# A Hyena convolution's spectra and inverses regrouped by even and odd times in a two-layer diffusion block

## The reference

```python
h = x * (1.0 + sc1) + sh1
q, k, v, z_hy, gate_a, gate_b = jnp.split(h @ lp['w_in'], SPLITS, axis=-1)
...
def bidir_long_conv(u, h, bias):
    L, C = u.shape[1], u.shape[2]
    g = jnp.concatenate([h[:, 0], jnp.zeros((1, C), jnp.float32), h[:0:-1, 1]], axis=0)
    U = jnp.fft.rfft(u, n=2 * L, axis=1)
    G = jnp.fft.rfft(g, n=2 * L, axis=0)
    y = jnp.fft.irfft(U * G[None], n=2 * L, axis=1)[:, :L]
    return y + u * bias
```

## Time and profile before

| what | value |
|---|---|
| median of 3 runs | 2062.82 us (2062.6 to 2062.84) |
| the profiled execution, its own time | 2061.39 us |
| its span, first to last instruction | 2059.6 us |
| mean granted TensorE clock | 0.992 of full |
| TensorE busy | 2016.4 us (98%), 13030 matmuls |
| VectorE busy | 1142.6 us (55%) |
| ScalarE busy | 747.6 us (36%) |
| GpSimd busy | 184.0 us (9%) |
| DMA | 207.07 MB, 101 GB/s over the span |

### The profile page before, as it was taken

How to read it: one execution, slowest core, us unless ns; L and a number is a source line. 1 busy time by engine, 2 the same in 40 slices (tenths; PEclk the granted TensorE clock), 3 DMA queues, 4 the chain that set the end, 5 groups by cost and what they waited for, 6 DMA issues and landing times.

```text
span 2059.6 us, 30339 instructions
## 1 busy us (share of the span) xinstructions
PE 2016.4 (98%) x13030; PEld 1917.8 (93%) x13030; DVE 1142.6 (55%) x1682; ACT 747.6 (36%) x1103; POOL 184.0 (9%) x202
## 2 busy tenths in 40 slices
PE   8999999999999999999999999999999999999997
PEld 3589998999989999999998999899998999999996
DVE  6416457777556767776545454863246433233435
ACT  3354453522264321333244443452226332133323
POOL 0120001200141000000031000120015000000011
PEclk9999999999999999999999998999999999999998
DMA  8331112254313335434322101222221212212121
GB/s 313 143 124 64 39 62 92 88 179 165 125 59 123 138 133 197 178 126 154 105 71 82 65 21 60 98 77 82 82 83 47 90 63 71 90 65 79 63 71 52
DMA packets 37726, 207.07 MB, mean 101 GB/s; under 512 B 4326, under 2 KB 7959, under 8 KB 18904
## 3 DMA queue, kind: packets, MB, share of 16 engines
q1 hardware_dynamic: 31192, 185.04, 25.1%
q0 software_dynamic: 3312, 13.35, 1.8%
q10 hardware_dynamic: 3088, 6.75, 0.9%
HBM read 196.98 MB, written 8.14 MB: 100 GB/s over the span
## 4 chain that ended last, share of the span: by engine, by line
PE 90%; DVE 4%; ACT 3%; issue 1%; DMA 1%; SPq 0%; POOL 0%; ACTq 0%; DVEq 0%
PE gemm_psum L609 50%; PE gemm_psum L639 15%; PE gemm_psum L662 3%; PE gemm_psum L682 3%; PE gemm_psum L622 3%; PE aux_psum L749 3%; PE aux_psum L802 2%; PE gemm_psum L788 2%; PE aux_psum L730 2%; PE gemm_psum L551 2%; PE gemm_psum L515 1%; PE aux_psum L738 1%; ACT h_src_rows L1174 1%; PE aux_psum L772 1%; DMA ada_early<-in_ada 1%
## 5 line engine op out<-in xcount | busy, mean ns | idle before, releaser
L609 PE MATMUL gemm_psum<-h_hi,w_hi 128*128 128x322 f32 x2144 | 497.2, 313 | 0.3
L609 PE MATMUL gemm_psum<-h_hi,w_lo 128*128 128x322 f32 x2144 | 493.5, 311 | 0.0
L609 PE MATMUL gemm_psum<-h_lo,w_hi 128*128 128x322 f32 x2144 | 492.1, 311 | 0.0
L609 PEld LDWEIGHTS gemm_psum<-h_hi,w_hi 128*128 128x128 f32 x2144 | 362.5, 189 | 4.4 <-issue 3.1
L609 PEld LDWEIGHTS gemm_psum<-h_lo,w_hi 128*128 128x128 f32 x2144 | 362.7, 189 | 0.0
L609 PEld LDWEIGHTS gemm_psum<-h_hi,w_lo 128*128 128x128 f32 x2144 | 362.2, 189 | 0.0
L1574 DVE TENSOR_TENSOR w_lo<-w_raw,w_hi 128x2048 fp32r<-128x2048 f32 (+3 forms) x130 | 251.3, 1933 | 198.7 <-ACT w_hi L1104 197.7
L1104 ACT ACTIVATE w_hi<-w_raw 128x2048 fp32r<-128x2048 f32 (+3 forms) x130 | 209.6, 1612 | 170.1 <-PE gemm_psum L639 65.6
L1562 DVE CUSTOM_DVE_ANT_0 aux_psum<-w_raw,cond_by_row 128x1024 f32<-128x1024 f32 x160 | 190.9, 1256 | 6.9 <-DMA w_raw<-in_ada_t 6.4
L1707 DVE SCALAR_TENSOR_TENSOR x<-gemm_psum,mod,x 128x128 f32<-128x128 f32 (+2 forms) x144 | 55.4, 434 | 157.8 <-PE gemm_psum L639 128.0
L639 PE MATMUL gemm_psum<-act_hi,w_lo 128*128 128x322 f32 x616 | 141.9, 311 | 0.0
(11 more groups left out here) (337 smaller groups left out, 3276.0 us busy)
## 6 DMA issues: line engine op xcount, KB each, us to landing
w_raw<-in_w_up SPq DMA_DIRECT2D x44, 1024.0 KB, 4.8
w_raw<-in_ada_t SPq DMA_DIRECT2D x40, 1024.0 KB, 4.7
w_raw<-in_w_down SPq DMA_DIRECT2D x32, 704.0 KB, 4.2
w_raw<-in_w_gate SPq DMA_DIRECT2D x16, 1024.0 KB, 4.7
w_raw<-in_w_z SPq DMA_DIRECT2D x12, 1024.0 KB, 4.7
w_raw<-in_w_out SPq DMA_DIRECT2D x8, 1024.0 KB, 4.7
g_kept<-g_rows_out POOLq DMA_DIRECT2D x10, 512.0 KB, 2.9
ada_early<-in_ada SPq DMA_DIRECT2D x4, 1024.0 KB, 20.4
```

Of the source, the lines that this page charges most:

```text
L609: last = mm(gp[:, 2 * (t % 2) + hf, 0:HALF], w[:, off + P * kk:off + P * (kk + 1)], moving(kk, lo)[:, hf * HALF:(hf + 1) * HALF], start=kk ...
```

## The change

The latent times are taken as four blocks by half (t below or from 256) and parity. The even-frequency inverses give 256 times. For the odd frequencies, only 4k + 1 is transformed directly, once from the even times (pair 3) and once from the odd times (pair 4), with two blocks each; their sum and difference are the two sets of odd spectra. The filter's odd spectra are combined in the same way, on GpSimd before they are stored. After the product with the filter, the two sets are again combined into an even-time and an odd-time part. Inverses are 256 columns wide and accumulate into two halves of a bank: a part that is equal for t and t + 256, and one that turns its sign; VectorE joins them. Chunk I1 is gone, and F1 comes ahead of I0. F0 has 12 blocks, F1 10 (with the context's inverse). The spectra 3 and 4 both run ahead of all latent inverses.

The diff, cut to its core:

```diff
-F0_BLOCKS, F1_BLOCKS = 14, 16
+F0_BLOCKS, F1_BLOCKS = 12, 10
-        + [("F", 0), ("pa", 0), ("I", 0), ("F", 1), ("I", 1)]
+        + [("F", 0), ("pa", 0), ("F", 1), ("I", 0)]
...
+    chunk_done[gF:gG] = [("usp_mm", 6), ("pa_mm", EARLY), ("usp_mm", 10), ("linv_mm", 4)]
-    EARLY_BANKS = [(1, 2), (1, 0), (1, 0), (0, 2)]
+    EARLY_BANKS = [(1, 2), (1, 0), (1, 2), (1, 0)]
-    G_V = [(0, 1), (2, 3), (4, 5), (6, 7, 8, 9), (6, 7, 8, 9)]
+    G_V = [(0, 1), (2, 3), (4, 5), (6, 8), (7, 9)]
...
+    def u_cols(b):
+        at = L0 + 2 * P * ((b - 1) // 2) + (b - 1) % 2
+        return CTX if b == 0 else slice(at, at + 2 * P - 1, 2)
...
-                    at = 512 * (2 * ((pair_ - 1) % 2) + o)
+                    at = 256 * (2 * (pair_ - 1) + o)
-                        last = mm(ax[:, j, :], y[:, ys, o, P * j:P * (j + 1)], w[slot][:, at:at + 512],
+                        last = mm(out(j), y[:, ys, o, P * j:P * (j + 1)], parts(w[slot][:, at:at + 256]),
...
+            for n in (2, 3):
+                pe.wait_ge(sem["pa_out"], due("pa_out", n - 1))
+                attn_projected(n)
+            pe.wait_ge(sem["w_split"], due("w_split", gF1 + 1))
             pe.wait_ge(sem["y_ready"], due("y_ready", 2))
...
+            pe.wait_ge(sem["us_rest"], due("us_rest", 4))
+            spectrum(3, U_V[3])
+            spectrum(4, U_V[4])
             pe.wait_ge(sem["w_split"], due("w_split", gI + 1))
             pe.wait_ge(sem["pa_out"], due("pa_out", 4))
+            for pair_ in range(1, PAIRS):
+                inverse(pair_, slot_of(gI), pair_ == 1, pair_ == PAIRS - 1)
...
+            act.wait_ge(sem["usp_mm"], due("usp_mm", 4))
+            split(gF1)
...
+                if p_ == 2:
+                    for o in range(2):
+                        act.wait_ge(sem["usp_mm"], due("usp_mm", 7 + o))
+                        run(ureg[:, 2 * o, :], spec_bank(6 + o), ACT.Copy).then_inc(sem["odd_out"], raised("odd_out"))
+                    split(gG)
...
+            split(gI)
+            dve.wait_ge(sem["cinv_mm"], due("cinv_mm", 1))
...
+            for o in range(2):
+                dve.wait_ge(sem["odd_out"], due("odd_out", o + 1))
+                dve.wait_ge(sem["usp_mm"], due("usp_mm", 9 + o))
+                first = ureg[:, 2 * o, :]
+                TT(ureg[:, 2 * o + 1, :], first, spec_bank(8 + o), ALU.subtract).then_inc(sem["usp_out"], raised("usp_out"))
+                dve.wait_ge(sem["usp_out"], now("usp_out"))
+                TT(first, first, spec_bank(8 + o), ALU.add).then_inc(sem["usp_out"], raised("usp_out"))
...
+            for at in range(2):
+                gr, gi = gsp[:, at, 0, :], gsp[:, at, 1, :]
+                ur, ui = ureg[:, at, :], ureg[:, 2 + at, :]
...
+                for to, a, b in ((prod[:, 0, :], ur, gr), (prod[:, 1, :], ui, gi), (us[:, 0, :], ur, gi), (us[:, 1, :], ui, gr)):
+                    TT(to, a, b, ALU.mult).then_inc(sem["dve_order"], raised("dve_order"))
+                dve.wait_ge(sem["dve_order"], now("dve_order"))
+                TT(ur, prod[:, 0, :], prod[:, 1, :], ALU.subtract).then_inc(sem["dve_order"], raised("dve_order"))
+                TT(ui, us[:, 0, :], us[:, 1, :], ALU.add).then_inc(sem["dve_order"], raised("dve_order"))
+            dve.wait_ge(sem["dve_order"], now("dve_order"))
+            for at, op in ((0, ALU.add), (1, ALU.subtract)):
+                for to, n in ((us, 2), (prod, 0)):
+                    TT(to[:, at, :], ureg[:, n, :], ureg[:, n + 1, :], op).then_inc(sem["y_src"], raised("y_src"))
+            for p_ in (3, 4):
+                for o in range(2):
+                    lo(ylo[:, Y_SLOT[p_], 1 - o, :], (us, prod)[o][:, p_ - 3, :], yhi[:, Y_SLOT[p_], 1 - o, :],
+                       "y_hi", 2 * p_ + o + 1, "y_ready")
             split(gG)
...
             for j in range(NHY):
-                STT(xu[:, j, LAT], xu[:, j, LAT], parc("hy_bias", j), ax[:, j, :], ALU.mult, ALU.add)\
+                rows = xu[:, j, LAT].rearrange("p (a t b) -> p a b t", a=2, b=2)
+                same, turned = (ax[:, j, 256 * a:256 * (a + 1)].rearrange("p (b t) -> p b t", b=2) for a in range(2))
+                for a in range(2):
+                    STT(rows[:, a], rows[:, a], parc("hy_bias", j), same, ALU.mult, ALU.add)\
+                        .then_inc(sem["dve_order"], raised("dve_order"))
+                dve.wait_ge(sem["dve_order"], now("dve_order"))
+                for a, op in ((0, ALU.add), (1, ALU.subtract)):
+                    TT(rows[:, a], rows[:, a], turned, op).then_inc(sem["dve_order"], raised("dve_order"))
...
+        def g_combine(l):
+            if l:
+                pool.wait_ge(sem["g_spill"], 16 * PAIRS)
+            pool.wait_ge(sem["gsp_out"], 10 * l + 6)
+            for o in range(2):
+                G.tensor_tensor(g_first[:, o, :], gst[:, 3, o, :], gst[:, 4, o, :], ALU.add).then_inc(sem["g_halves"], 1)
+            pool.wait_ge(sem["g_halves"], 4 * l + 2)
+            for o in range(2):
+                G.tensor_tensor(gst[:, 4, o, :], gst[:, 3, o, :], gst[:, 4, o, :], ALU.subtract).then_inc(sem["g_halves"], 1)
+            pool.wait_ge(sem["g_halves"], 4 * l + 4)
```

More of the change, by code:

```diff
@@ L345, in _program @@
         h2T = sb("h2T", [P, NT], F32, s)
-        feat = sb("feat", [FEAT, NT], F32, s)
+        with ExitStack() as s2:
+            feat = sb("feat", [FEAT, NT], F32, s2)
+        g_first = sb("g_first_half", [P, 2, HY_W], F32, s)
         dreg = sb("d_block", [P, 2, HY_W], F32, s)
@@ L547, in g_spectrum @@
                 for kb, pl in enumerate(places):
[L548 removed]
+                    blk = 4 * (pair_ % 3) + 2 * o + kb
                     cols_ = slice(P * blk, P * (blk + 1))
@@ L784, in spectrum @@
                 for kb, pl in enumerate(places):
-                    blk = (4 * pair_ + 2 * o + kb) if pair_ < 3 else (8 * (pair_ - 3) + 4 * o + kb)
+                    blk = 4 * (pair_ % 3) + 2 * o + kb
                     cols_ = slice(P * blk, P * (blk + 1))
@@ L794, in inverse, with out @@
             ys = Y_SLOT[pair_]
+            parts = lambda ap: ap if pair_ < 3 else ap.rearrange("p (a t) -> p a t", a=2)
+            def out(j):
+                if pair_ < 3:
+                    return ax[:, j, 256 * (pair_ - 1):256 * pair_]
+                return ax[:, j, :].rearrange("p (a b t) -> p a b t", a=2, b=2)[:, :, pair_ - 3, :]
             for o in (1, 0):
@@ L1323, in _ @@
                     early_row(1)
-                    split(gI)
                 if p_ == 1:
@@ L1835, in _ @@
             split(gA)
-            for p_ in range(PAIRS):
+            for p_ in range(3):
                 gr, gi = gsp[:, G_SLOT[p_], 0, :], gsp[:, G_SLOT[p_], 1, :]
@@ L1871, in _ @@
-                if p_ == 3:
-                    split(gI1)
+                if p_ == 0:
+                    split(gF1)
+            split(gI)
+            dve.wait_ge(sem["cinv_mm"], due("cinv_mm", 1))
+            for j in range(NHY):
+                STT(xu[:, j, CTX], xu[:, j, CTX], parc("hy_bias", j), ax[:, 2, P * j:P * (j + 1)],
+                       ALU.mult, ALU.add).then_inc(sem["cinv_out" if j == 3 else "dve_order"], raised("cinv_out" if j == 3 else "dve_order"))
+            for o in range(2):
[5 more added lines that the diff above has]
+                TT(first, first, spec_bank(8 + o), ALU.add).then_inc(sem["usp_out"], raised("usp_out"))
@@ L2084, in _ @@
                         h_lo(0, h, d)
-                        if h == 0 and d % 2:
-                            g_spill(1, d // 2 + 1)
+                        if d == KD - 1:
+                            if h:
+                                g_combine(1)
+                            for n in (1, 2) if h else (3, 4):
+                                g_spill(1, n)
             pool.wait_ge(sem["h_ready"], due("h_ready", 2 * KD))
@@ L2189, in _dft_constants @@
     k4 = np.arange(P)
+    two = [2 * np.arange(P) + b for b in range(2)]
     lat = []
@@ L2192, in _dft_constants @@
         re, im = forward(4 * k4 + add, DEC_SEQ // 2, N)
+        br, bi = back(4 * k4 + add, DEC_SEQ // 2, N)
         if add == 0:
@@ L2195, in _dft_constants @@
             im[:, 0] = np.cos(np.pi * np.arange(DEC_SEQ // 2))
-        lat += [re[:P], re[P:], im[:P], im[P:]]
-        br, bi = back(4 * k4 + add, DEC_SEQ, N)
-        if add == 0:
             br[0] /= 2
-            bi[0] = np.cos(np.pi * np.arange(DEC_SEQ)) / N
-        i0 += [br, bi]
-    f0 = ctx + lat + cinv
-    f1 = []
-    for o in range(2):
-        fr = 2 * (P * o + np.arange(P)) + 1
-        re, im = forward(fr, DEC_SEQ, N)
-        f1 += [m[P * b:P * (b + 1)] for m in (re, im) for b in range(4)]
-        i1 += list(back(fr, DEC_SEQ, N))
+            bi[0] = np.cos(np.pi * np.arange(DEC_SEQ // 2)) / N
+        lat += [m[rows] for m in (re, im) for rows in two]
+        i0 += [m[:, cols] for m in (br, bi) for cols in two]
+    f0 = ctx + lat
+    re, im = forward(4 * k4 + 1, DEC_SEQ, N)
+    br, bi = back(4 * k4 + 1, DEC_SEQ, N)
```

(16 more changed lines are left out.)

57 lines of the change are left out of this document (18 added, 39 removed).

## The result

| | time, us | executions |
|---|---|---|
| kernel before | 2062.71 (2061.13 to 2062.84) | 4 |
| kernel after | **2034.09** (2032.39 to 2035.55) | 4 |
| ratio | 0.9863, 95% interval 0.9846 to 0.988 | |

The profiled execution of after took 2032.39 us, its span is 2030.4 against 2059.6: 29.2 less.

What follows compares the result with a forecast made beforehand. TensorE, with 90% of the chain, was taken as the bound until ScalarE or VectorE became last. Filter stage -9.9, opening -0.8 and two layers at -2 gave -14.7 us: 2048 us, range 2036 to 2058.

Steps and rivals of the forecast that it cites:

- Filter stage: Filter spectra before the layers: ScalarE's 1.81 us per row becomes the bound, first projection at 101.6 instead of 111.58, -9.9 us.
- Hyena stretches: Each layer's Hyena stretch and gate multiplication: TensorE loses 16.5 us, but the layer wins only 2 us (1.2 to 3).
- The serial chain: Hyena stretch, VectorE: 20 new operations of 128x512 that combine the odd spectra, 12.8 us, ending at 358.4.
- the idle time: Hyena stretch, TensorE: nothing to do from inverses 1 and 2 (350.3) until 359.1, 8.8 us.
- a join: Hyena stretch, VectorE: each residual operation becomes half-width multiply-adds, a wait and additions, 1.6 us instead of 0.66.
- 381.9 against 383.1: Gate multiplication, layer 0: time in us when h row 7 is ready, forecast for after against the kernel before.
- The clock: Hyena stretch: half of inverses 3 and 4 run at the low level after the 8.8 us gap, costing nothing.
- The F loads shrink: Opening loads: 0.13 and 0.39 MB less and shorter VectorE splits of F, -0.8 us (0 to -1.5).
- (a): Rival, whole kernel: TensorE's saved time comes out whole, 44 us less, 2019 us; chance 0.06.
- (b): Rival, before the layers: clock falls in TensorE's pauses or GpSimd's adds hold VectorE, 6 us lost, about 2055 us; chance 0.14.
- (d): Rival, gate multiplication: clock falls after the 8.8 us gap and stays at 1.2 GHz, +10 per layer, 2072 us; chance 0.07.
- (c): Rival, layers: halved residual operations and strides cost whole ones, 4 to 5 us more per layer, 2058 to 2061; chance 0.07.

Runs made afterwards that it cites:

- f_again: Kernel before with the odd filter spectra summed over two blocks of times instead of four, run a second time: 2044.54 us.
- b_again: Kernel before, unchanged, for a second profiled execution: 2061.45 us.
- f_only: Kernel before with the odd filter spectra summed over two blocks of times instead of four, first run: 2045.57 us.
- a_f14: Kernel after with each layer's first F block 1792 columns wide again instead of 1536: four executions 2039.12 to 2040.33 us, two 2032.89 and 2033.30.
- pe_only: Kernel before with only TensorE's part of the change in the layers (two-block odd spectra, 256-column inverses): median 2050.71 us.

## Why the prediction was wrong

**Filter stage: right.** With the opening, -10.7 was forecast and 11.0 measured (f_again: 10.0 without the opening's 1.0); so were ScalarE's pace of 1.81 us per row and copy and its start at 83.84 (84.9 forecast). The sum written down gives -10.0 where -9.9 stands. GpSimd's work cost nothing (39.65 us with and without it, as shown above).

**The first projection, -1.5, not seen, and partly chance.** The earlier trace rows hold the low clock of 112 to 117 us, and I read it only as evidence on what gaps do, not as time to be won. In after it falls at 95.7 us, where TensorE waits for ScalarE anyway. But in b_again it fell before the projection in the kernel before too, so that the 1.5 us tell where it fell in one execution, and not what the change does.

**Hyena stretches: the mechanism right, the size off.** The serial chain (12.8 forecast, 13.05 measured), the idle time (8.8; 8.0), its releaser, a join (1.6; 1.58) are as worked out. The term that failed is the arrival of row 7, "381.9 against 383.1": counted from the first spectrum it was put at 68.7 us, and came at 66.5. Of the 2.2 us, 1.2 were already won when VectorE reached row 2 (52.8 instead of 54.0; my schedule had VectorE's pairs that much later), and row 2 to row 7 took 13.8 instead of 14.7. Over two stretches, the gain was 8.35 us where 4 were forecast: 4.3 us missed.

**The clock: the step that failed most.** The prediction asked only what the new 8.8 us gap would do, in the Hyena stretch, and put that at nothing, which held: 6.8 us at the low level in layer 0 fell mostly into the gap, the last inverses took 7.1 us instead of 5.7, behind which VectorE's row 2 ended later still, and in 352 to 370 us the clock was 1.00. It never asked what the low clock already in the trace of before cost, a term that it left at nothing without a reason. One fall of 13.7 us stood in layer 1 and none in the same work of layer 0; it was worth 6.5 us, and in the kernel after it hung on 0.25 us in each of two splits. "The F loads shrink" was costed only in the opening; the same blocks are loaded and split again in each layer, ahead of copies that TensorE waits for: 0.5 us per layer (0.35 net: the strided transposes, for which 1.5 was allowed, cost 0.15), plus the fall.

Together: 6.5 and 1.5 for the clock, 4.35 for the stretches, 0.7 for the splits, and the rest (1.4, of it 0.85 at the end, where the clock also varies from execution to execution) make the 14.5 us missed.

**The base.** Three executions within 0.24 us looked firm, but the kernel has two levels 7.4 us apart. Against the lower one, 14.7 forecast stand against 21.2.

**Rivals.** (a), TensorE's time whole, is refuted by the TensorE-only run: 2.4 for 16.5, at most 4.0 if the clock had stayed up. (b) and (d) did not come: pauses under ScalarE's pace brought the low clock once or twice there, and the first projection started at 100.5 to 102.0 us in the profiles of after and its variants, some 1.5 us apart and not 6; the gate multiplication stayed at the full clock. (c) did not come either: a join took 1.58 us, and not the 2.7 of four whole operations. The Trainium skill, "TensorE: Matmul & The Clock Gate", section "Why this matters for your kernels", has the clock drop for idle gaps between bursts; the 8.0 us gap agrees, and the fall in layer 1 does not look like such a one, since its longest pause was 1.22 us. The Trainium skill, "TensorE: Matmul & The Clock Gate", section "A second HAM failure mode: psum-queue depth-cycling", tells of short idles between groups of matmuls, frequent ones, that make the clock go up and down; here pauses of 0.2 and 1.2 us were enough and one of 1.0 us was not, which agrees in kind, though they are not many.

**Open:** at which times the pauses matter. In before, pauses that come 8.0 and 10.6 us earlier (the profiles of f_only and f_again) or 1.8 us later bring no fall, 0.6 us changes nothing, and in a_f14, 17 us earlier, it falls as well. In pe_only the long pause ended 0.9 us earlier than in before and the profile has no fall; whether its two slowest executions, 6 and 9 us above the median, had one is not known. No run shows the rule behind these times.

## What to carry to other kernels

List every stretch at the low clock in the trace of before, with what it costs and what TensorE waited for ahead of it, before costing a change: a change that shortens such a wait, or only moves it, can win or lose several us far from its own place. Compare with the mean clock of every execution at hand, since a kernel can have two levels and a few executions may show one. And where TensorE is busy throughout a stretch and VectorE for 80% of it, do not take VectorE's idle time for what TensorE can save there: of 16.5 us saved, 2.4 to 4.0 came out, though VectorE was idle for 12. Follow VectorE's queue with what it waits for instead. What VectorE is spared counts in full until TensorE's own stream is the bound again.

## What was not expected of the hardware

A delay need not make a kernel slower: with 1.8 us of matmuls in vain, twelve executions of before took 2056.3 us in the mean, 2.2 less than the 23 beside them, since none took the time of the upper level (by the interval of the ratio, 0.9977 to 1.0001, just not clear of no change; that the upper level is gone is clear, none of 12 against 13 of 23). And 0.25 us of split work on each of two engines decided over 6.5 us: with 1792 columns, 4 of 6 executions of after took the time of a fall to half clock for 13.7 us, with 1536 none of 8. What the low level costs: the same work took 21.37 us in layer 1 of before with the fall and 14.85 in layer 0 without it.
